# Two-layer hybrid decoder trunk: VectorE folds the planes of squares of every RMS norm before TensorE sums them over the partitions

## What is computed

```python
def rms_norm(x, w):
    xf = x.astype(jnp.float32)
    y = xf * lax.rsqrt(jnp.mean(xf * xf, axis=-1, keepdims=True) + EPS)
    return (y * w.astype(jnp.float32)).astype(x.dtype)

for i in range(DEPTH):
    hn = rms_norm(h, norm_mix_pre[i])
    m = deltanet_stickbreak_mixer(hn, ...) if i % 2 == 0 else s5_mixer(hn, ...)
    h = h + rms_norm(m, norm_mix_post[i])
    hn = rms_norm(h, norm_ffn_pre[i])
    h = h + rms_norm(swiglu_ffn(hn, ...), norm_ffn_post[i])
```

## Time and profile before

| | us |
|---|---|
| median of 3 runs | 3546.03 |
| the 3 runs | 3544.58, 3546.03, 3550.68 |
| span of the profiled execution | 3530.7 |

### The profile page before, as it was taken

The page is one execution under the profiler, slowest core; times in us unless marked ns, Lnnn a source line. Parts: engine busy times, 40 slices in busy tenths (PEclk is TensorE's granted clock), DMA queues, the critical chain, the costliest instruction groups (busy, mean ns, idle before and its releaser), DMA issues.

```text
span 3530.7 us, 46227 instructions
## 1 busy us (share of the span) xinstructions
PE 3044.9 (86%) x18053; PEld 2842.5 (81%) x18053; DVE 1377.5 (39%) x2293; ACT 746.2 (21%) x1347; POOL 933.9 (26%) x390
## 2 busy tenths in 40 slices
PE   4999877866679699999999785775997999999996
PEld 3999866754459599999999585564995999999995
DVE  3650155535640623223322665664005323223324
ACT  2221234425541311011011221222002111011011
POOL 2444300000004034435434122000342334435430
PEclk9999999977779899999999996555997999999999
DMA  4122210001002211111111322122113111111112
GB/s 145 69 99 96 96 39 27 24 6 37 18 18 73 83 37 60 48 36 48 48 48 37 119 62 61 36 47 50 36 48 121 36 36 59 48 36 50 46 34 96
DMA packets 121966, 195.16 MB, mean 55 GB/s; under 512 B 7344, under 2 KB 91824, under 8 KB 121648
## 3 DMA queue, kind: packets, MB, share of 16 engines
q1 hardware_dynamic: 54544, 113.99, 10.7%
q10 hardware_dynamic: 67360, 80.33, 6.7%
HBM read 150.45 MB, written 43.84 MB: 55 GB/s over the span
## 4 chain that ended last, share of the span: by engine, by line
PE 76%; DVE 11%; ACT 6%; issue 3%; ACTq 1%; DMA 1%; DVEq 0%; SPq 0%
PE bank L500 20%; PE bank L501 20%; PE bank L502 20%; PE bank L547 4%; PE bank L681 2%; PE bank L902 1%; PE bank L903 1%; DVE area L1661 1%; PE bank L673 1%; ACT area L945 1%; DVE area L1466 1%; DVE area L1609 1%; PE bank L792 1%; PE bank L882 1%; PE bank L904 1%
## 5 line engine op out<-in xcount | busy, mean ns | idle before, releaser
L500 PE MATMUL bank<-x_hi,w_hi 128*128 128x344 f32 (+2 forms) x3600 | 1159.1, 322 | 47.1 <-DVE x_lo L1836 16.3
L501 PE MATMUL bank<-x_lo,w_hi 128*128 128x344 f32 (+2 forms) x3600 | 1157.8, 322 | 0.0
L502 PE MATMUL bank<-x_hi,w_lo 128*128 128x344 f32 (+2 forms) x3600 | 1153.1, 320 | 0.0
L472 POOL TENSOR_TENSOR w_hi<-stage,const 128x1024 fp32r<-128x1024 f32 x193 | 468.6, 2428 | 2476.5 <-PE bank L502 2459.8
L500 PEld LDWEIGHTS bank<-x_hi,w_hi 128*128 128x128 f32 x3600 | 680.3, 189 | 51.7 <-issue 29.2
L502 PEld LDWEIGHTS bank<-x_hi,w_lo 128*128 128x128 f32 x3600 | 680.5, 189 | 0.0
L501 PEld LDWEIGHTS bank<-x_lo,w_hi 128*128 128x128 f32 x3600 | 679.4, 189 | 0.7
L476 POOL TENSOR_TENSOR w_lo<-stage,w_hi 128x1024 fp32r<-128x1024 f32 x193 | 469.2, 2431 | 15.1
L1637 DVE TENSOR_TENSOR area<-area,bank 128x352 f32<-128x352 f32 (+1 forms) x132 | 68.0, 515 | 778.7 <-ACT area L1277 778.7
L500 PE MATMUL bank<-act_hi,w_hi 128*128 128x344 f32 (+1 forms) x1056 | 341.0, 323 | 0.0
L502 PE MATMUL bank<-act_hi,w_lo 128*128 128x344 f32 (+1 forms) x1056 | 338.8, 321 | 0.0
(11 more groups left out here) (214 smaller groups left out, 2805.3 us busy)
## 6 DMA issues: line engine op xcount, KB each, us to landing
stage<-wstream SPq DMA_DIRECT2D x193, 512.0 KB, 3.4
proj<-area ACTq DMA_DIRECT2D x28, 520.0 KB, 2.6
area<-proj ACTq DMA_DIRECT2D x40, 256.0 KB, 4.3
resid<-area ACTq DMA_DIRECT2D x6, 1376.0 KB, 6.4
area<-resid ACTq DMA_DIRECT2D x6, 1376.0 KB, 10.3
area<-proj ACTq DMA_DIRECT2D x12, 520.0 KB, 4.5
area<-xT ACTq DMA_DIRECT2D x4, 1376.0 KB, 10.4
resid<-area ACTq DMA_DIRECT2D x3, 1408.0 KB, 5.7
```

Of the source, the lines that this page charges most:

```text
L472: pool.tensor_tensor(per_block(w_hi[:, slot, :]), per_block(stage[:, h, :]), all_ones, ALU.mult).then_inc(high_split, 1)
L500: mm(out[:, 0:n], w_hi[:, slot, wk], hi[:, xk, a:a + n], start=first, stop=False)
L501: mm(out[:, 0:n], w_hi[:, slot, wk], lo[:, xk, a:a + n], start=False, stop=False)
L502: return mm(out[:, 0:n], w_lo[:, slot, wk], hi[:, xk, a:a + n], start=False, stop=last)
```

## The change

ScalarE's squares are as before. VectorE now adds the four planes of a half into one row with a tensor_reduce over the plane axis, into `rs` of that event (`fold_squares`), and signals `nm_folded`. TensorE does one ones-matmul for each half, on that row, and signals `nm_sum`. The second fold of an event waits for the first half's matmul, since it writes the same row. A ScalarE square still waits for `nm_sum` as before.

```diff
-                    for k in range(KT):
-                        if k % 4 == 0:
-
-                            pe.wait_ge(nm_square, 2 * e + k // 4 + 1)
-                        last = mm(norm_bank(r, c, m)[:, 0:n], ones, nv["sq"][:, k % 4, 0:n], start=(k == 0),
-                                  stop=(k == KT - 1))
-                        if k % 4 == 3:
-                            last.then_inc(nm_sum, 1)
+                    for half in range(2):
+                        pe.wait_ge(nm_folded, 2 * e + half + 1)
+                        mm(norm_bank(r, c, m)[:, 0:n], ones, nv["rs"][e % 2][:, 0:n], start=(half == 0),
+                           stop=(half == 1)).then_inc(nm_sum, 1)
...
+            def fold_squares(r, c, m):
+
+                e, n = norm_event(r, c, m), CUTS[c][1]
+                for half in range(2):
+                    dve.wait_ge(nm_square, 2 * e + half + 1)
+                    if half:
+                        dve.wait_ge(nm_sum, 2 * e + 1)
+                    V.tensor_reduce(out=nv["rs"][e % 2][:, 0:n], in_=nv["sq"][:, :, 0:n].rearrange("p k t -> p t k"),
+                                    axis=mybir.AxisListType.X, op=add).then_inc(nm_folded, 1)
+
...
-                for c, m in norm_steps(r):
+                steps = norm_steps(r)
+                fold_squares(r, *steps[0])
+                for at, (c, m) in enumerate(steps):
+                    if r > 0 and at + 1 < len(steps):
+                        fold_squares(r, *steps[at + 1])
...
                         last.then_inc(nm_normed, 1)
+                        if r == 0 and at + 1 < len(steps):
+                            fold_squares(r, *steps[at + 1])
                         dve.wait_ge(nm_high, p + 1)
```

More of the change, by code:

```diff
@@ L317, in trunk @@
         nm_square = sem("nm_square")
+        nm_folded = sem("nm_folded")
         nm_root = sem("nm_root")
```

## The result

The changed kernel takes 3673.99 us in the median of 4 runs (3659.89 to 3681.77), the kernel before 3548.36 in 4 (3544.58 to 3554.2). The ratio is 1.0353, with a 95% interval of 1.033 to 1.0375: 126 us slower, and the forecast was 109 us slower with 3655 as the time.

The account below looks back on a forecast made before the run. VectorE's last body was taken to end every norm stage. Stages 0 to 4 add 6.6 + 28.7 + 32.3 + 26.5 + 14.9 = +109 us, giving 3655 us, range 3611 to 3687.

Parts of the forecast that it names:

- The round trip: Between an event's two folds in the norm stages: VectorE idle for ones-matmul 1.5 and second square 1.4 us.
- The ones-matmul: One ones-matmul for each half in the norm stages: 1.5 us at the low clock, 0.9 at the other end.
- The hidden tile: TensorE's tile before the sums of (2,1), stages 1 to 3: 8.0 to 10 us, hidden by 1.6 us.
- The fold, mis-sized: Each of 48 added VectorE tensor_reduces in the norm stages: taken as 2.1 us, bounds 1.6 and 2.7.
- The row that I took: Profile row of 32-element tensor_tensors, one input strided: 194 ns against 184, 0.31 ns an element more; gave the 2.1 us fold.
- The row of 1040 elements: Profile row L1836, one input and the output strided: 2060 ns, 1.84 ns an element; would give a 2.7 us fold.
- first rival: In the norm stages, VectorE's idle time swallows the folds: faster, -43 us, time 3503; chance 0.02.
- third: Rival for the norm-stage folds: they run at the contiguous rate, +85 us, time 3631; chance 0.22.
- fourth: Rival: GpSimd's weight splits hold up the first folds of stages 0, 1, 3: +15, time 3670; slow-fold cases together 0.25.
- second: Rival: norm-stage folds as slow as the strided write, 2.7 us: +138, time 3684; chance 0.25 together with GpSimd holding up folds.
- The check on the method: Same accounting for stages 1 to 3 before: opening 10.4 plus bodies 63.8 give 74.2; 8 to 14 us above are waits.
- (a) of the prediction: Lower bound for a fold: contiguous tensor_tensor rate, 1.04 ns an element and 0.15 us fixed, so 1.6 us.

Follow-up runs that it names:

- the contiguous run: The changed kernel with each fold reading as many elements in one contiguous piece of the buffer (wrong sums); single run 3646.26 us, stages 435.4 us.

## Why the prediction was right, and by how much it was off

- **Which wait ends last.** All five stages end with VectorE's last body, in the changed kernel as before, and the sum by stages, 129 us, is what the medians show (126).
- **The round trip.** Idle time of VectorE inside a pair of folds was put at 3 us and is 2.99 to 3.11, except for three pairs of 2.32 behind the hidden tile, whose ones-matmul takes 0.85. That it stands in front of a ready body, and would be gone with another order, was worth 57 us in the run with folds inside the body, 58 by the same accounting.
- **The ones-matmul.** 1.5 us at the low clock: the square starts 1.56 us after the matmul (1181.44 to 1183.00), and the window over it has a granted clock of 0.50 (the number behind the busy times), the 1.2 GHz level:

```profile
1181.40:1183.00 1.60, 1.52 (x2) 0.50 (x2) 0.00 (x0) 0.00 (x1) 0.00 (x0) 0.50 0.48 154
```
- **The hidden tile.** I had it start at 74.4 us and end 1.6 us before the fold that it must precede. It starts 78.7 us into the stage and takes 10.5, and the ones-matmul behind it was released by the fold after 2.42 us idle. It stayed hidden.
- **The fold, mis-sized.** The term was 2.1 us and it is 2.48 for 344 columns and 2.55 for 352. Over 48 folds 0.41 us each are 20 us, and 109 + 20 = 129: the whole miss lies here. With the mean of 2.51 in place of 2.1 the accounting gives 478 for the stages, and 478.9 was measured. The row that I took, 10 ns more for a strided input in 32 elements, has half the price that the folds show (0.31 against 0.65 ns an element). I had noted that it can be read to 2 ns, which is too little to make up the gap; why operations of 32 elements show only half of the price no run explains. The row of 1040 elements, at 1.84 ns each, was the nearer in size, and 2.7 us the nearer end.
- **The rivals.** VectorE's idle time did not swallow the folds (first rival): its idle time grew, from 26.6 to 34.3 us in stage 2, since the waits moved. The fold at the contiguous rate (third) is out by the source view, and would have given stages of 435, which is what the contiguous run measured. GpSimd did not hold up the reduces (fourth): beside a split they cost at most 0.07 us more. The slow fold (second) was right in direction and too high by 0.2 us a fold; with 138 us it was nearer to the measured 126 than my 109.
- **TensorE idle before it resumes** was put at some 14 us and is 13.52; the first reciprocals were put 19 us after the first square and come at 21.0, which is four folds of 0.4 us more. The 14 us stand without a working in the prediction, and nothing in its sum hangs on them.
- **The check on the method.** I put the 8 to 14 us that the stages of before stand above its bodies down to waits for ones-matmuls alone. In stages 1 and 3 one scalar_tensor_tensor beside a split took 2.10 and 2.43 us for 0.57, so 1.5 and 1.9 us of them were that. In the changed kernel the bodies start later and none is slowed.

## What to carry to other kernels

Work given to an engine with a low busy share costs its full time, and the wait that it brings as well, when that engine's queue sets the end of the stage: look at what stands behind the new instruction, not at the share. Issue the two halves of a handshake around work that is ready, never in front of it (57 us here, for the same instructions). And where a short chain waits for a few matmuls of another engine, first make each of them shorter, before moving them.

## What the runs showed of the hardware

- A tensor_reduce of float32 over 1376 elements takes 1586 ns with steps of 4 or 8 bytes and 2586 from 16 bytes on; 1408 bytes are no worse (2482 ns). With 0.15 us as the fixed part, as in (a) of the prediction, these are 1.04 and 1.7 to 1.8 ns an element, an estimate.
- A tensor_tensor with both inputs in SBUF beside GpSimd's splits went from 0.52 to 2.54 us, and the split from 2.34 to 2.99; a scalar_tensor_tensor with two such inputs went from 0.57 to 2.66 us; a tensor_reduce at the same place lost at most 0.07 us of 2.53.
- The stretch between stages 0 and 1, with identical code, took from 1059 to 1086 us in eleven profiles. So a difference of less than 1% between two single profiles of this kernel says nothing as a whole, while the sums of the norm stages of the two profiles of before agree to 1.1 us.
